# The gate of a hybrid GLA and convolution layer, from eight steps of 256 columns to four steps of 512 columns with streamed weights

## What is computed

```python
n = rmsnorm(x)                                # x: 4096 tokens x 1024
z = n @ W_in                                  # q, k, v, gates, conv channels
y = [gated linear attention ; short gated conv]
h = x + y @ W_out
gate = sigmoid(h @ W_g + b_g)                 # 1024 x 1024
h = h + gate * (p @ W_ple)                    # p: 4096 x 256
out = rmsnorm(h)
```

## Time and profile before

| | us |
|---|---|
| median of 3 runs | 2001.32 (2001.08 to 2004.48) |
| profiled execution, its own time | 2001.79 |
| its span, first to last instruction | 2000.0 |
| TensorE busy | 1971.0, 99% |
| gate, first matmul to last | 1569.8 to 1987.6 |
| granted TensorE clock, mean | 0.999 |

### The profile page before, as it was taken

The page is one execution under the profiler, slowest core; times in us unless marked ns, Lnnn a source line. Parts: engine busy times, 40 slices in busy tenths (PEclk is TensorE's granted clock), DMA queues, the critical chain, the costliest instruction groups (busy, mean ns, idle before and its releaser), DMA issues.

```text
span 2000.0 us, 28845 instructions
## 1 busy us (share of the span) xinstructions
PE 1971.0 (99%) x11232; PEld 1711.9 (86%) x11232; DVE 1357.3 (68%) x1574; ACT 783.3 (39%) x1230; POOL 693.3 (35%) x759
## 2 busy tenths in 40 slices
PE   6999999999999999999999999999999999999998
PEld 5788888888888888888888888888888999999998
DVE  6765876768654685685685675685585577777776
ACT  5444454444433432332332323323223255455544
POOL 4766665767661132332232321264652000000000
PEclk9999999999999999999999999999999999999999
DMA  6345445354447322227422137485586912222222
GB/s 239 130 171 191 162 155 209 116 199 166 170 163 316 147 92 95 88 96 298 159 90 89 64 106 282 177 311 192 190 295 250 368 69 93 82 86 78 95 96 85
DMA packets 89905, 322.84 MB, mean 161 GB/s; under 512 B 11664, under 2 KB 24384, under 8 KB 78784
## 3 DMA queue, kind: packets, MB, share of 16 engines
q1 hardware_dynamic: 56928, 185.46, 25.4%
q0 software_dynamic: 32864, 135.85, 18.6%
HBM read 193.34 MB, written 127.93 MB: 161 GB/s over the span
## 4 chain that ended last, share of the span: by engine, by line
PE 91%; DVE 5%; issue 1%; ACT 1%; DMA 1%; SPq 0%; DVEq 0%; ACTq 0%
PE bank L1304 15%; PE bank L1298 15%; PE bank L1300 15%; PE bank L997 7%; PE bank L1001 7%; PE bank L998 7%; PE bank L1386 5%; PE bank L1384 5%; PE bank L1389 4%; PE bank L1437 2%; PE bank L1436 2%; PE bank L1435 2%; DVE XL L1973 1%; PE bank L1394 1%; PE bank L1122 1%
## 5 line engine op out<-in xcount | busy, mean ns | idle before, releaser
L1298 PE MATMUL bank<-XH,WC 128*128 128x512 f32 x1344 | 524.5, 390 | 0.3 <-DVE u L2214 0.2
L1304 PE MATMUL bank<-XL,WC 128*128 128x512 f32 x1344 | 523.1, 389 | 0.2 <-DVE XL L2139 0.2
L1300 PE MATMUL bank<-XH,WC 128*128 128x512 f32 x1344 | 522.9, 389 | 0.0
L2139 DVE TENSOR_TENSOR XL<-RQ,XH 128x1024 fp32r<-128x1024 f32 x168 | 217.2, 1327 | 221.4 <-ACT XH L1705 220.0
L1304 PEld LDWEIGHTS bank<-XL,WC 128*128 128x128 f32 x1344 | 252.3, 188 | 53.0 <-DVE XL L2139 0.7
L1298 PEld LDWEIGHTS bank<-XH,WC 128*128 128x128 f32 x1344 | 252.4, 188 | 52.9 <-DVE u L2214 0.6
L1300 PEld LDWEIGHTS bank<-XH,WC 128*128 128x128 f32 x1344 | 252.4, 188 | 51.6
L1386 PE MATMUL bank<-XHg,WC 128*128 128x256 f32 x896 | 246.2, 283 | 0.0
L1384 PE MATMUL bank<-XHg,WC 128*128 128x256 f32 x896 | 246.2, 283 | 0.0
L1705 ACT ACTIVATE XH<-RQ 128x1024 fp32r<-128x1024 f32 x168 | 170.7, 1053 | 168.8 <-PE bank L1304 150.1
L1389 PE MATMUL bank<-XLg,WC 128*128 128x256 f32 x672 | 190.2, 283 | 0.0
(11 more groups left out here) (248 smaller groups left out, 3837.7 us busy)
## 6 DMA issues: line engine op xcount, KB each, us to landing
WC<-w_scratch SPq DMA_DIRECT2D x28, 2048.0 KB, 9.6
RQ<-n_scratch POOLq DMA_DIRECT2D x32, 1024.0 KB, 5.4
w_scratch<-prep_hi POOLq DMA_DIRECT2D x84, 256.0 KB, 2.3
w_scratch<-PB POOLq DMA_DIRECT2D x84, 256.0 KB, 2.3
n_scratch<-raw SPq DMA_DIRECT2D x8, 2048.0 KB, 7.2
y_scratch<-y_sb SPq DMA_DIRECT2D x64, 256.0 KB, 2.8
RQ<-y_scratch POOLq DMA_DIRECT2D x16, 1024.0 KB, 5.6
xt<-xb_dram SPq DMA_DIRECT2D x64, 256.0 KB, 4.8
```

What stands on the lines that cost most here:

```text
L1298: nc.tensor.matmul(bank[:], WC[:, i, q, 0, k], xh, start=(k == 0 and i in (P1, P2, P5)), stop=False, skip_group_check=True)
L1300: nc.tensor.matmul(bank[:], WC[:, i, q, 1, k], xh, start=False, stop=False, skip_group_check=True)
L1304: mm = nc.tensor.matmul(bank[:], WC[:, i, q, 0, k], xl, start=False, stop=(k == 3), skip_group_check=True)
L2139: nc.vector.tensor_tensor(XL[:, k], RQ[:, OPERAND[s % 7], 2 * h:2 * h + 2], XH[:, k].bitcast(F32), ALU.subtract).then_inc(sx_lo, 1)
```

## The change

The gate becomes four steps (g = 12 to 15, p = 0 to 3) of the twelve steps' form: pairs of blocks, `RQ` loaded by GpSimd from the stored h, 512-column products in `A_BANK`, and the machinery of `block_hi`, `block_lo`, `make_t2`, `make_t4`, `copy_sum`. What differs from those steps:

- P2, P5 and P3 have two banks (`C_RING`) instead of four; P5 and P3 alternate in pairs of tiles. Behind each tile of P2, P5, P3 and P4 stands one `ple_unit` of 6 matmuls of 512 columns, in two more banks (`PLE_RING`); the unit waits until the one two before it has been multiplied (`g_scaled`).
- `WC` keeps three chunks. Each product's 2 MB of weights is loaded again in every pair, when the product three before has ended (`stream_weights`). The freed space holds h for the residual in five groups of 1 MB (`load_res`), p, and W_ple. h is stored as output from there.
- GpSimd sums the squares (`add_squares`), half of them in the next pair. The means of a pair are taken in the next pair's P1 and P6 (`out_stats`), and VectorE normalises there.
- In step 11 GpSimd issues the loads of Q12 and Q11 for the gate, then the last two parts of the gate's weights, then Q22, then the two tiles of W_ple, then Q21, and then makes t3.
- At the end, TensorE runs two `ple_unit`s ahead of P4, and VectorE's two normalisations are of 512 columns.

The diff, cut to its core (in ScalarE's `gate` the copies, sigmoids and squares are spread in the same order as VectorE's steps):

```diff
...
+ALL_STEPS = STEPS + NP
+RING = 3
+RES = 5
...
+C_RING = (6, 3)
+PLE_RING = (4, 7)
...
+                for n in range(4, 12):
+                    store_h(first + n)
                 for c in range(8):
                     sp.wait_ge(rows_stored[c], 16 * 2 * (NP - 1))
...
+                sp.wait_ge(sx_free, 4 * (7 * g + P2 + 1))
+                sp.wait_ge(sx_free, 4 * (7 * g + P5 + 1))
+                for n in range(3):
+                    load_res(n)
+                sp.wait_ge(sx_free, 4 * (7 * g + P3 + 1))
+                load_res(3)
+                load_p(0, 0)
+                load_p(0, 1)
+                sp.wait_ge(tile_stored, 16 * 2 * (STRIPS + PLE_K))
                 sp.wait_ge(sx_free, 4 * (7 * g + P4 + 1))
                 for part, tile in enumerate((WPH, WPL)):
                     sp.dma_start(tile[:].bitcast(F32), g_scratch[part].rearrange("p (k m c) -> p k m c", k=PLE_K, m=KT)
                                  ).then_inc(wp_loaded, 16)
...
+            def load_res(n):
+                if n >= RES:
+                    sp.wait_ge(out_stored[n % RES], h_count + 16 * (n // RES))
+                sp.dma_start(res_group(n), group_of(h_scratch, n)).then_inc(res_loaded[n % RES], 16)
+            def store_out(n, normalised):
+                sp.wait_ge(out_norm, normalised)
+                sp.dma_start(group_of(out, n), res_group(n)).then_inc(out_stored[n % RES], 16)
...
+            def stream_weights(p, i):
...
+                sp.wait_ge(sx_free, 4 * (7 * (STEPS + p) + i - RING + 1))
+                if p == 0 and i == P5:
+                    wait_prepared(sp, 4)
+                sp.dma_start(WC[:, gate_place(p, i)].bitcast(F32),
+                             w_scratch[3, i].rearrange("p (q h k c) -> p q h k c", q=4, h=2, k=4)).then_inc(w_chunk[i], 16)
+            def gate(p):
+                if p > 0:
+                    load_p(p, 0)
+                    store_out(4 * (p - 1) + 1, 16 * (p - 1) + 4)
+                    store_out(4 * (p - 1) + 2, 16 * (p - 1) + 8)
+                stream_weights(p, P2)
+                if p > 0:
+                    store_out(4 * (p - 1), 16 * (p - 1) + 12)
+                    store_out(4 * (p - 1) + 3, 16 * (p - 1) + 16)
+                stream_weights(p, P5)
+                if p > 0:
+                    load_res(4 * p + 2)
+                    load_res(4 * p + 3)
+                    load_res(4 * p + 1)
+                else:
                     for c in range(8):
...
+                load_res(4 * p + 4)
+                stream_weights(p, P3)
+                stream_weights(p, P4)
+                stream_weights(p, 7 + P1)
+                load_p(p + 1, 1)
+                stream_weights(p, 7 + P6)
+                stream_weights(p, 7 + P7)
...
-                else:
+                elif g < STEPS - 1:
                     gate_parts(g, 0)
-                if g == STEPS - 1:
-                    for n in range(PLE_K):
-                        prep_tile(n)
                 split_waits(s + P6)
...
+                if g == STEPS - 1:
+                    for c in range(8):
+                        pool.wait_ge(rows_stored[c], 16 * 2)
                 split_waits(s + P7)
                 load_quadrant(g + 1, Q12)
                 split_waits(s + P5)
                 load_quadrant(g + 1, Q11)
-                if g in GATE_SLOTS:
+                if g == STEPS - 1:
+                    gate_parts(g, 0)
+                elif g in GATE_SLOTS:
                     gate_parts(g, 1)
                 split_waits(s + P3)
                 pool.wait_ge(t1_made, 2 * (g + 1))
                 load_quadrant(g + 1, Q22)
-                if g in GATE_SLOTS:
+                if g == STEPS - 1:
+                    for n in range(PLE_K):
+                        prep_tile(n)
+                elif g in GATE_SLOTS:
                     gate_parts(g, 2)
...
+            for p in range(NP):
+                g = STEPS + p
+                s = 7 * g
+                pool.wait_ge(rq_loaded[Q12], 16 * (g + 1))
+                pool.wait_ge(rq_loaded[Q22], 16 * (g + 1))
+                difference(g, Q12, Q12, t3_made)
+                if p > 0:
+                    add_squares(p - 1, range(8, 16))
+                split_waits(s + P6)
+                pool.wait_ge(t4_made, 2 * (g + 1))
+                difference(g, Q11, Q11, t1_made)
+                if p < NP - 1:
+                    split_waits(s + P7)
+                    load_quadrant(g + 1, Q12)
+                    split_waits(s + P5)
+                    load_quadrant(g + 1, Q11)
+                add_squares(p, range(4))
+                if p < NP - 1:
+                    split_waits(s + P3)
+                    pool.wait_ge(t1_made, 2 * (g + 1))
+                    load_quadrant(g + 1, Q22)
+                add_squares(p, range(4, 8))
+                if p < NP - 1:
+                    split_waits(s + P4)
+                    load_quadrant(g + 1, Q21)
+            add_squares(NP - 1, range(8, 12))
...
+                elif i == P2 and q < 2 and p == 0:
+                    pe.wait_ge(c_out, c12(STEPS - 1, q))
+                elif i == P2 and q < 2:
+                    pe.wait_ge(g_sum, sums_to(p - 1, 2, q + 2))
+                    pe.wait_ge(out_root, 2 * p)
+                elif i == P2:
+                    pe.wait_ge(g_sum, sums_to(p, 0, q - 2))
+                elif i == P5 and q < 2:
+                    pe.wait_ge(g_sum, sums_to(p, 0, q + 2))
+                elif i == P5:
+                    pe.wait_ge(g_sum, sums_to(p, 2, q - 2))
+                else:
+                    pe.wait_ge(g_sum, sums_to(p, 1, q))
...
+                pe.wait_ge(p_lo, 2 * p + t + 1)
+                if n < 2:
+                    pe.wait_ge(c_out, c12(STEPS - 1, 2 + n))
                 else:
-                    pe.wait_ge(g_scaled, n - 2)
...
+            def gate(p):
+                g = STEPS + p
+                def with_ple(c, q):
+                    product_tile(g, PRODUCT[c], q, None)
+                    ple_unit(p, c, q)
+                product_tile(g, P1, 0, None)
+                if p > 0:
+                    out_stats(p - 1, 1)
...
+                for q in range(4):
+                    with_ple(0, q)
+                for two in range(2):
+                    for c in (1, 2):
+                        with_ple(c, 2 * two)
+                        with_ple(c, 2 * two + 1)
+                if p < NP - 1:
+                    for q in range(4):
+                        with_ple(3, q)
+                    return
+                ple_unit(p, 3, 0)
+                ple_unit(p, 3, 1)
+                product_tile(g, P4, 0, None)
+                product_tile(g, P4, 1, None)
+                out_stats(p, 1)
+                ple_unit(p, 3, 2)
+                product_tile(g, P4, 2, None)
+                ple_unit(p, 3, 3)
+                product_tile(g, P4, 3, None)
+                last_stats()
...
+                block_lo(s + 7)
+                make_t2(g + 1)
...
+            def gate(p):
+                if p == 0:
+                    add_products(g - 1, 3, P4, range(3))
+                    block_lo(s + 1)
+                    add_products(g - 1, 3, P4, range(3, 4))
+                else:
+                    gate_mix(p - 1, 14)
+                    block_lo(s + 1)
+                    gate_mix(p - 1, 15)
+                    final_norm(p - 1, 1, (1,))
+                    total_split(p - 1, 0)
+                    final_norm(p - 1, 1, (2,))
+                block_lo(s + 2)
+                if p > 0:
+                    final_norm(p - 1, 0)
+                block_lo(s + 3)
+                make_t4(g)
+                split_p_lo(p, 0)
+                split_p_lo(p, 1)
+                block_lo(s + 4)
+                gate_sum(p, 0)
+                for u in range(1, 4):
+                    gate_sum(p, u)
+                    gate_mix(p, u - 1)
+                block_lo(s + 5)
+                gate_mix(p, 3)
+                gate_sum(p, 4)
+                for u in range(5, 12):
+                    gate_sum(p, u)
+                    gate_mix(p, u - 1)
+                    if u == 9:
+                        block_lo(s + 6)
+                gate_mix(p, 11)
+                block_lo(s + 7)
+                if p < NP - 1:
+                    gate_mix(p, 12)
+                    make_t2(g + 1)
+                    gate_mix(p, 13)
+                    total_split(p, 1)
                     return
+                total_split(p, 1)
+                gate_mix(p, 12)
+                gate_mix(p, 13)
+                final_norm(p, 1, (1,))
+                gate_mix(p, 14)
+                final_norm(p, 1, (2,))
+                gate_mix(p, 15)
+                final_norm(p, 0)
...
```

More of the change, by code:

```diff
@@ L96 @@
 SMALL = 7
-STAT = 5
 H_SCALED, H_DONE = 1, 2
@@ L1491, in _ @@
                 step(g)
-            for b in range(NB):
-                gate(b)
-            last_stats()
+            for p in range(NP):
+                gate(p)
```

798 lines of the change are left out of this document (321 added, 477 removed).

## The result

The changed kernel takes 2010.74 us (median of 5 runs, 2007.84 to 2013.42) beside 2001.32 for the kernel before (median of 5 runs, 2001.08 to 2004.48): a ratio of 1.0044, 95% interval 1.0033 to 1.0056. It is slower by 9 us where 5 us faster were forecast, and it lies above the range of 1985 to 2009. Its profiled execution has a span of 2008.9 us against 2000.0.

The account below looks back on a forecast made before the run. The prediction took TensorE's matmul rate plus the end to bound the kernel. Its terms, -23.0 + 8.5 + 1.5 + 4 + 3.7 = -5.3 us, took 2001.8 to 1996.5 us, with a range of 1985 to 2009.

Parts of the forecast that it names:

- TensorE's work: In the gate, 3456 matmuls of 256 columns become 1728 of 512, a gain of 23.0 us.
- The way in: At the gate's start, TensorE idles 8.5 us because GpSimd's late W_ple tiles delay t3, t2 and the bank-emptying adds.
- The clock: Behind the idle stretch at the gate's start, TensorE returns at 1.2 GHz for some 3 us, costing 1.5 us.
- Inside the pairs: Within the gate's pairs, single waits from VectorE and GpSimd hindering each other cost 1 us per pair, 4 us.
- Streamed weights: In the gate's pairs, reloaded weights land in time despite nearly full queues; cost 0, bounds 0 and 6 us per pair.
- The end: From the last product to the kernel's end, 16.1 us against 12.4, a cost of 3.7 us (2 to 6).
- (d): At the way in, both tiles take 35 us under full DMA, losing all 23 us; 2003 to 2006, chance 0.06.
- (b): Inside the pairs, two-bank rings and shared access cost 16 us instead of 4; 2008.5, chance 0.18.
- (a): At the way in, t3 comes by 1568, so nothing waits and the clock stays; 1984.5, chance 0.17.
- (c): In the gate's pairs, weights come late, 3 x 3 to 3 x 6 us; 2005 to 2014, chance 0.09.

Follow-up runs that it names:

- e9b: e8 with the gate's three first weight loads spread: one behind the stored W_ple tiles, the others behind four output-row stores each; 1978.94 us, ratio 0.9888.
- e4: Changed kernel with SyncE's residual loads and first two p loads issued behind the W_ple loads; 2004.18 us, ratio 1.0017 to the kernel before.
- e2: Changed kernel with step 11's two weight parts and both W_ple tiles back ahead of t1 on GpSimd; 1990.98 us, ratio 0.9947.
- e5: e2 with each t3 of the gate made as two separate GpSimd steps, a hand-over to itself behind each half; 1984.72 us, ratio 0.9923.
- e3: Changed kernel with GpSimd making the gate's first t3 ahead of the W_ple tiles, weight parts still late; 1999.33 us, ratio 0.9991.
- e7: e2 with the gate's first weights loaded only when both W_ple tiles are stored; 1995.37 us, ratio 0.9970.
- e6: Changed kernel with only step 11's two weight parts back ahead of t1, W_ple tiles still behind Q22's load; 2001.79 us, ratio 1.0006.
- e8: e5 and e7 together: two-step t3 and the gate's first weights behind the stored tiles; 1987.78 us, ratio 0.9936.
- e1: Changed kernel with VectorE's t2 for the gate's first pair behind the adds that empty step 11's P4; 2000.79 us, ratio 0.9999.

## Why the prediction was wrong

- **TensorE's work, -23.0: right.** -22.8 in the changed kernel, as summed above, and -23.7 in e9b, where nothing else is in the way. The price from matmul distances in the same trace held. The Trainium skill (TensorE: Matmul & The Clock Gate, "Back-to-back issue gap") gives 2.5 ns above N / 2.4 for a single matmul; by that the gain would have been an estimated 4.3 us, and these runs show five times as much.
- **The way in, +8.5: the step that failed**, at 23.3 (bounds 2 to 16). Chain, place and releasers were right. The failed step is "Both W_ple tiles take 23.3 us at least ... each may take one to three us more, so I take 1571 (1566 to 1578)". The tiles began at 1546.25, 2 us later than I took, behind weight parts of 16.2 us where I took 10.4; they took 35.6 us and ended at 1581.8. I took a duration from a stretch with a DMA share of 0.40 into one with 0.91, though rows 3 showed a share of 0.97 for 1549 to 1562 already. Of the 14.8 us excess 10.8 are the tiles' end, 3.0 come because TensorE is done with step 11 at 1566.8 instead of 1569.8, and 0.9 are t2 and the add. e4 assigns 8.2 us of the stall to the residual and p loads alone. e2 takes all of it away by the order, with tiles of 32.2 us: the late place makes a stall possible, and the traffic at that place gives it a good part of its size.
- **The clock, +1.5:** 2.6, in the bounds; 13 matmuls at the 1.2 GHz level.
- **Inside the pairs, +4:** 5.4. That the size was near is luck, for the place was not right: nothing is lost from P2 to P5; the four waits (three of 1.7 to 1.8 us and one of 0.2) are all at the W_ple unit behind P3's end, which I had named second. e5 shows the mechanism.
- **Streamed weights, 0:** right in the changed kernel. In e3 they were the bound, but behind a wait on SyncE. The demand was forecast well, and the limit was not: a pair of the changed kernel moves 281 GB/s with a DMA share of 0.71 only (1679 to 1779), and the 324 GB/s that I took for full is no ceiling, since e7 moves 407.
- **The end, +3.7:** 2.4, inside its bounds. VectorE's last mix ends at T + 3.0, not T + 3.7.
- **The rivals.** (d) had the right duration, 35 us, and the right piece; its 2003 to 2006 lacked the clock's 2.6 us and the pairs' 5.4. I gave it 0.06 because I weighed it as a mishap of the forecast and not by the DMA share in rows 3. (b) gave a time near the result, 2008.5, by another cause, worth 5 us here and not 16. That its number is near is no merit of it. (a) and (c) did not occur.

What stays open: how the 23 us would divide if the transfers of the first tile too ran alone. The gate's first three weight loads are not what held it up in the changed kernel: the last is issued 23 us ahead of it, and they land within 9.0 us.

```profile
L517 SPq DMA_DIRECT2D WC<-w_scratch x3: 320/326/326, 1501.7 to 1523.5; - x3
DMA to landing us min/median/max: 7.8/8.7/9.0
```

Beside the first tile SyncE stores and loads row tiles and GpSimd loads Q22; e4 leaves these as they are, and the window 1547 to 1560 has a share of 0.99 there too. No run took them away at the late place, and e4 and e6 overlap.

## What to carry to other kernels

A chain that alternates short work and transfers (load, round, store, load) has no duration of its own: before it is moved, read the DMA share of the stretch it leaves and of the one it enters, since here each wait of 3.4 to 4.3 us became 7 to 9. Look for what stands behind its waits on every queue. Spread a burst of loads instead of moving it: moved it cost 4 us (e7), spread it gave 9 (e9b against e8). Where VectorE adds two SBUF tiles beside a long run of GpSimd, try a gap in that run: a hand-over between two halves gave 6 us.

## What was not expected of the hardware

- One VectorE mix lasted 6.46 us through three GpSimd instructions without a gap between them; with a hand-over between the first two it was 2.98.
- A stall of 3.1 us (e2) was followed by a granted clock of 0.70 in 1540 to 1545, and one of 6.1 us (e7) by 0.66 in 1556 to 1561. The pairs' waits of 1.7 to 1.8 us left it at 1.00 in the changed kernel, and yet one of them, the third pair's of 1.8 us, was followed by 0.67 in e1, e4 and e6.
- The share of 0.91 that doubled the tiles' waits came with 340 GB/s, and e7 shows 1.00 with 407. GpSimd's wait for the same load of 512 KB was 3.38 us before the change, 7.55 in the changed kernel and 3.00 in e4: what runs beside it set the wait, not its own size.
